# Fp32r products of a two-block transformer kernel that visit their moving columns in other orders

## What is computed

```python
def chunk(args):
    hc, ec, gc = args
    u = peer_u[ec]
    a = jax.nn.gelu(jnp.einsum("ckd,cd->ck", u, hc).astype(jnp.float32)) * gc
    vv = peer_v[ec]
    return jnp.einsum("ck,ckd->cd", a.astype(vv.dtype), vv)
```

```python
up = causal_dwconv(h2 @ w_up[l], ffn_conv_w[l], ffn_conv_b[l])
gate_h, val_h = jnp.split(up, 2, axis=-1)
x = x + (jax.nn.gelu(gate_h, approximate=True) * val_h) @ w_down[l]
```

## Time and profile before

| what | us |
|---|---|
| median of 2 runs (1598.95 and 1600.56) | 1599.76 |
| span of the profiled execution, first to last instruction | 1595.2 |
| TensorE matmuls busy | 1583.0 |
| TensorE weight loads busy | 1493.5 |
| VectorE busy | 1071.3 |
| GpSimd busy | 885.8 |
| ScalarE busy | 884.2 |

### The profile page before, as it was taken

The page is one execution under the profiler, slowest core; times in us unless marked ns, Lnnn a source line. Parts: engine busy times, 40 slices in busy tenths (PEclk is TensorE's granted clock), DMA queues, the critical chain, the costliest instruction groups (busy, mean ns, idle before and its releaser), DMA issues.

```text
span 1595.2 us, 33476 instructions
## 1 busy us (share of the span) xinstructions
PE 1583.0 (99%) x12568; PEld 1493.5 (94%) x12568; DVE 1071.3 (67%) x1867; ACT 884.2 (55%) x1251; POOL 885.8 (56%) x413
## 2 busy tenths in 40 slices
PE   9999999999999999999999999999999999999998
PEld 8999899999999999998888888889999999999998
DVE  7998643779933777778888666776937383455521
ACT  6557766454454444444444445457676654666653
POOL 8786468868886000000000244457876689888886
PEclk9999999999999999999999999999999999999999
DMA  6565346555555555555555666666543356666653
GB/s 222 171 191 154 106 132 187 186 175 190 188 184 186 171 171 171 172 169 171 179 178 166 215 190 194 195 189 185 172 148 106 109 177 185 188 190 187 191 187 119
DMA packets 86218, 277.03 MB, mean 174 GB/s; under 512 B 11233, under 2 KB 18161, under 8 KB 86129
## 3 DMA queue, kind: packets, MB, share of 16 engines
q1 hardware_dynamic: 85712, 274.76, 54.9%
q0 software_dynamic: 272, 1.05, 0.2%
q10 hardware_dynamic: 144, 0.00, 0.0%
HBM read 274.73 MB, written 1.05 MB: 173 GB/s over the span
## 4 chain that ended last, share of the span: by engine, by line
PE 93%; issue 2%; DVE 2%; POOL 1%; ACT 1%; DMA 0%; SPq 0%; DVEq 0%; ACTq 0%; POOLq 0%
PE gemm L679 36%; PE gemm L982 22%; PE gemm L684 18%; PE aux L1268 4%; PE gemm L813 3%; PE aux L962 2%; POOL w_lo L462 1%; PE gemm L700 1%; PE gemm L725 1%; PE gemm L1268 1%; PE aux L932 0%; PE gemm L799 0%; ACT w_hi L1364 0%; PE gemm L706 0%; PE gemm L742 0%
## 5 line engine op out<-in xcount | busy, mean ns | idle before, releaser
L462 POOL TENSOR_TENSOR w_lo<-raw,w_hi 128x1024 fp32r<-128x1024 f32 (+1 forms) x330 | 791.7, 2407 | 294.7 <-ACT w_hi L1364 285.6
L1364 ACT ACTIVATE w_hi<-raw 128x1024 fp32r<-128x1024 f32 (+1 forms) x492 | 515.8, 1050 | 575.5 <-PE gemm L679 324.0
L679 PE MATMUL gemm<-h_lo,w_hi 128*128 128x256 f32 x2144 | 294.3, 279 | 0.0
L679 PE MATMUL gemm<-h_hi,w_hi 128*128 128x256 f32 x2096 | 293.3, 282 | 0.4 <-ACT w_hi L1364 0.3
L684 PE MATMUL gemm<-h_hi,w_lo 128*128 128x256 f32 x2096 | 288.6, 280 | 1.4 <-POOL w_lo L462 0.9
L679 PEld LDWEIGHTS gemm<-h_lo,w_hi 128*128 128x128 f32 x2144 | 268.9, 188 | 0.3 <-issue 0.2
L679 PEld LDWEIGHTS gemm<-h_hi,w_hi 128*128 128x128 f32 x2096 | 264.0, 188 | 3.3 <-issue 1.6
L462 DVE TENSOR_TENSOR w_lo<-raw,w_hi 128x1024 fp32r<-128x1024 f32 x162 | 196.6, 1222 | 104.3 <-ACT w_hi L1364 103.7
L684 PEld LDWEIGHTS gemm<-h_hi,w_lo 128*128 128x128 f32 x2096 | 262.8, 188 | 3.5 <-POOL w_lo L462 2.2
L982 PE MATMUL gemm<-w_hi,act_parts 128*128 128x512 f32 x1008 | 250.9, 391 | 0.4 <-ACT act_parts L1565 0.4
L982 PEld LDWEIGHTS gemm<-w_hi,act_parts 128*128 128x128 f32 x1008 | 188.0, 188 | 39.0 <-issue 0.5
(11 more groups left out here) (436 smaller groups left out, 2065.6 us busy)
## 6 DMA issues: line engine op xcount, KB each, us to landing
raw<-in_w_u SPq DMA_DIRECT2D x128, 512.0 KB, 3.6
raw<-in_w_ev SPq DMA_DIRECT2D x128, 512.0 KB, 3.7
raw<-in_w_up SPq DMA_DIRECT2D x48, 512.0 KB, 4.3
raw<-in_w_gate SPq DMA_DIRECT2D x24, 512.0 KB, 3.8
raw<-in_w_down SPq DMA_DIRECT2D x24, 512.0 KB, 4.0
raw<-in_w_conv_in SPq DMA_DIRECT2D x16, 512.0 KB, 4.6
raw<-in_w_peer_q SPq DMA_DIRECT2D x16, 512.0 KB, 3.5
raw<-in_w_branch SPq DMA_DIRECT2D x24, 288.0 KB, 2.9
```

What stands on the lines that cost most here:

```text
L462: eng.tensor_tensor(w_lo[v][:, 0:n], raw[c.raw][v][:, 0:n], w_hi[v][:, 0:n], ALU.subtract).then_inc(lo_ready[v], 1)
L679: mm = pe.matmul(out, w[:, k, :], act_part[:, k, :], start=(n == k == 0), stop=False)
L1364: act.activation(w_hi[v][:, 0:n], raw[c.raw][v][:, 0:n], ACT.Copy).then_inc(hi_ready[v], 1)
```

## The change

It adds `strided` and `falling`, which give another view of the same columns, three tables of such views, and `column_order`, which picks one by the place of the chunk in its round and by the tile. The same view is put on the product and on the moving operand of each matmul, so every column gets what it got before, in another order. `strided(groups, run)` visits runs of `run` neighbouring columns, with a step of `groups * run` from one to the next, and then the next group; `down=True` takes the runs of a group from the end. `falling(run)` takes all runs from the end to the start. `lambda x: x` leaves the order as it was: that is tile 0 of the first chunk of each round of scores. The helper gives the old order for all other chunks that go through `product_tile`.

```diff
+        def strided(groups, run, down=False):
+
+            def turn(tile):
+                v = tile.rearrange("p (j g c) -> p g j c", g=groups, c=run)
+                return v[:, :, ::-1, :] if down else v
+            return turn
+
+        def falling(run):
+
+            return lambda tile: tile.rearrange("p (j c) -> p j c", c=run)[:, ::-1, :]
+
+        SCORE_ORDER = ((lambda x: x, strided(4, 4)), (strided(8, 4), strided(16, 4)),
+                       (strided(2, 8), strided(4, 8)), (strided(2, 16), falling(4)))
+        UP_ORDER = ((strided(4, 4, True), strided(2, 8, True)), (strided(8, 8), strided(4, 16)),
+                    (strided(2, 32), strided(2, 4, True)), (falling(8), falling(16)))
+        VALUE_ORDER = ((strided(4, 4), strided(2, 4)), (strided(8, 4), strided(2, 8)),
+                       (strided(4, 8), strided(4, 16)), (falling(4), strided(2, 16)))
+
+        def column_order(c, v):
+
+            for name, orders in (("u", SCORE_ORDER), ("up", UP_ORDER), ("ev", VALUE_ORDER)):
+                first = plan[name][0].index
+                if first <= c.index < first + len(plan[name]):
+                    return orders[(c.index - first) % BANKS][v]
+            return lambda x: x
...
                 w = by_k(w_hi[v], m, n=steps)
+                turn = column_order(c, v)
...
-                        mm = pe.matmul(out, w[:, k, :], act_part[:, k, :], start=(n == k == 0), stop=False)
+                        mm = pe.matmul(turn(out), w[:, k, :], turn(act_part[:, k, :]), start=(n == k == 0), stop=False)
...
-                    mm = pe.matmul(out, w[:, k, :], x[0][:, k, :], start=False, stop=(k == steps - 1))
+                    mm = pe.matmul(turn(out), w[:, k, :], turn(x[0][:, k, :]), start=False, stop=(k == steps - 1))
...
             def expert_values(c, it, opens=False):
                 for v in range(2):
+                    turn = column_order(c, v)
...
-                                mm = pe.matmul(gemm[2 * half + tt][:, :], a[:, c.raw, v, tt * P:(tt + 1) * P],
-                                               w[v][:, half * (D // 2):(half + 1) * (D // 2)],
+                                mm = pe.matmul(turn(gemm[2 * half + tt][:, :]), a[:, c.raw, v, tt * P:(tt + 1) * P],
+                                               turn(w[v][:, half * (D // 2):(half + 1) * (D // 2)]),
```

## The result

The changed kernel takes 1622.97 us (two runs, 1622.8 to 1623.14) against 1599.76 us before: a ratio of 1.0151 on record, 95% interval 1.0132 to 1.0171 (the two medians alone give 1.0145). That is 23 us slower: inside the range of 1590 to 1690, but outside the forecast's own range of 1594 to 1612, and far from its figure of no cost. The span went from 1595.2 to 1620.7 us.

The account below looks back on a forecast made before the run. TensorE was taken to bind, time being the matmul count times their start-to-start pitch. Span 1595.2 + 0 for the new orders, plus 4.6 us around the span, gave 1599.8 us, with a range of 1590 to 1690.

Parts of the forecast that it names:

- the forecast's own range: Whole kernel: 1594 to 1612 us if no cost counts, given a chance of 0.77.
- the counts (2688, 1104, 1512): Matmuls given a new order in scores, ups and values; at the old pitches 785 us, half of the span.
- I take nothing: Scores, ups and values: a column not beside the last one was priced at no cost, so the span stays at 1595.2 us.
- rival 1: Edited matmuls: each jump between runs stalls the array one cycle of 0.417 ns, giving 1690 to 1724 us; chance 0.10.
- the nearest row: L962, building the gate planes: its hopping reads cost 3.9 ns over column time, taken to speak for stepped reads at full rate.
- The bounds, -58 and +727 us: Edited matmuls: all time over column time goes, or each column of a stepped write costs two array cycles.
- Rival 2: Products of the edited matmuls: stepped writes run at half rate, +727 us, 2327 us; chance 0.05.
- Rival 3: Edited matmuls: only some orders collide, such as groups from the end at double column time, +151 us, 1751 us; chance 0.04.
- Rival 4: Edited matmuls: another order avoids a collision that the old one has, 1541 us if all goes; chance 0.04.

Follow-up runs that it names:

- e2: Changed kernel with only the product written in the new orders and the moving operand read side by side: 1597.98 us, ratio 1.0001 to before.
- e4: Changed kernel with padding altered so that h_hi and h_lo lie 8 bytes further on: 1627.95 us.
- e3: Changed kernel with other orders in all three tables, including runs of 2 and longer steps, both sides turned: 1898.49 us in one run.
- e5: Changed kernel with h_hi and h_lo 64 bytes further on, what lies behind h_lo moving too: 1627.22 us.
- e6: Changed kernel with h_hi and h_lo 32 bytes further back: 1628.57 us.
- e8: Changed kernel with all tiles from the first weight tile on, h_hi and h_lo included, moved together 32 bytes further on: 1623.34 us.
- e7: Changed kernel with strided(4, 4) in all 256-column products of product_tile and of down, values side by side: 1580.89 us, ratio 0.9889.
- e10: e7 with strided(4, 4) in the values too: 1577.62 us, ratio 0.9864.
- e9: Changed kernel with only score moving reads stepped, runs of 4 at steps of 64 to 128 columns; products, ups, values in old order: 1612.94 us.

## Why the prediction was right or wrong

**The bound was read rightly.** TensorE carries the whole difference, 25.7 of 25.5 us, the pitch from start to start is where it shows, and the counts (2688, 1104, 1512) add up to it with the measured pitches. No other engine had a part.

**The step that failed is "I take nothing".** The price of a column that is not beside the last one was put at zero and measured at 11.0 + 12.0 + 2.4 = 25.4 us. That the measured time lies within 1590 to 1690 all the same is luck: the range was drawn up to rival 1's lower figure, and rival 1 doesn't hold either. The step went wrong in the choice of the nearest row. L962 reads every second 16-bit element, so its hop is 4 bytes, and the pair of elements that it needs lies within 8 bytes; `falling(2)` at 117.7 ns and `(2, 2)` at 228.2 suggest that what matters is whether an access goes on next to the last or leaves the neighbourhood. That row said nothing of steps of 32 to 256 bytes. The bounds, -58 and +727 us, did hold the answer. The dearest order of the scores, at +16.8 ns, also broke the mark that the prediction set itself (any score pattern over 125 ns).

**Rival 1**, a cycle for each jump, has the wrong rule. `(4, 4)` and `(16, 4)` both have 64 runs and differ by 18.4 ns. A price near one cycle a step turned up, but only in runs of 4 with steps of a multiple of 64 columns.

**Rival 2** is refuted where it stood: e2 steps all products and takes 1.0001 of before's time. Of the two sentences on PSUM in the Trainium skill ("Advanced Engine Details and Errata", Memory Cachelines), the one by which any pattern that isn't contiguous slows matmuls significantly doesn't hold for these orders, with runs from 4 to 32 columns. Its sentence for SBUF, that a line needs two hits for full performance, agrees with e4, where half lines make two hits each and cost nothing more. By the prediction's count a run of 2 also makes two hits, and by the other PSUM sentence a pair of neighbours is enough; yet e3 took 217 to 236 ns for 117 with runs of 2 on both sides. So by that count one of these two sentences doesn't hold here, and no run shows which.

**Rival 3**, only some orders collide, comes nearest, with a chance of 0.04 and the wrong class and size. It named backward groups at double time, +151 us. The falling orders cost 1 to 3 ns in scores and ups (`falling(4)` to `falling(16)`) and 6.5 in the values. The prediction named long steps beside them, with sums of that size too; they did rise, but by 16.8 ns at most in the scores and not by 107, and all steps of 64 columns together make some 10 of the 25.4 us.

**Rival 4**, a gain from another order, was held off with the argument that the pitch is the same while the other engines' work differs. That speaks against collisions with their accesses, but not with TensorE's own weight reads, which are the same everywhere. e5, e6 and e8 show that the place of `h` against other tiles moves the pitch, and e7 and e10 that there was a gain: 22 us in e10. The bound of 58 us counted scores, ups and values alone, and these became 5.9, 2.0 and 2.3 us shorter in e10, 10 us; the rest came from products that the change had left alone.

Open: why `(4, 4)` is the better one in the scores at every place of `h` tried (114.7 to 115.7) is not settled; that it meets the weight reads less is argued, not shown. Its form from the end had 115.0 ns in the ups of the changed kernel, but 118.8 in those of e4. The ups of e9, in the old order and with all tiles in their old places, stand at 117.7 ns for 116.8, which nothing here explains. The values pay for steps of 8 to 32 columns too (231.5 to 245.3), and their 12 us were not taken apart.

## What to carry to other kernels

Where matmuls bind, the way in which the moving operand is read has a price per hop: keep runs of at least 16 bytes, and with such short runs avoid steps of 128 bytes and of multiples of 256, while a product in runs of 4 or more columns cost nothing in any order tried. Take a pattern's price from the start-to-start pitch of each pattern, since a mean over a line mixed -1.6 and +16.8 ns here. When a row of the trace stands in for an operation that it doesn't show, ask first whether it shares the quantity that the price may hang on: here the distance of the hop in bytes.

## What the runs showed of the hardware that was not expected

- An fp32r matmul that reads runs of 4 columns with a step of 16 is faster than one that reads side by side: 114.8 for 116.7 ns at 256 columns, 225.5 for 226.7 at 512; 1.4% of this kernel (e10).
- The pitch of a side-by-side matmul moves between 116.8 and 119.8 ns when its moving operand lies elsewhere in SBUF against the other tiles (e5, e6), and is untouched when all move together (e8). It can also change by 1 to 5 ns with no operand of it moved (ups of e9, values of e4).
- Stepped reads of 4 columns are dear at 256 bytes and at twice that: 133.4 and 133.6 ns at steps of 256 and 512 bytes, 114.6 to 119.7 at the six steps between (e9).
- Stepped runs of 2, on both sides, about double the time (217 to 236 ns at 256 columns), but pairs visited backwards as neighbours don't (117.7) (e3).
